# Sample attention of a hybrid decoder step: scores in the key matmuls, inverse key roots on GpSimd

## The chip, the cores and the metric

The kernel runs on one core of a Trainium2 chip, in one launch. The metric is the device time of that core in microseconds. The engines are named here as TensorE (PE in the profile; PEld are its weight loads), VectorE (DVE), ScalarE (ACT), GpSimd (POOL) and SyncE (SP).

## The reference

One inference step of a decoder layer over 1024 prompt tokens (plus 16 meta tokens) and over 8 running sequences of 8 new tokens each, which have 4096 cached positions. The part that this case is about is the attention of the sample tokens. Cached are latents `c` of 256 numbers and rotary keys `kr` of 32 numbers per position, in pages of 128 positions that a table names. For each of 8 heads:

```python
k_nope = einsum('tr,rhd->thd', c_all, w_uk)            # 64 per head
k = rms_norm(concat([k_nope, broadcast(kr_all)]), gain) # 96 per head
s = einsum('qhd,khd->hqk', q, k) * SCALE                # masked to past positions
p = softmax(s)
ctx = einsum('hqk,kr->qhr', p, c_all)                   # over latents
out = einsum('qhr,rhv->qhv', ctx, w_uv)
```

with `rms_norm(x) = x * rsqrt(mean(x*x) + 1e-6) * gain`. Everything is float32.

## The kernel before, in words

The program runs stage after stage, each a block that all engines leave together: constants, the front of the sample tokens (`front`), `sample_prepare`, `sample_attention`, `sample_values`, then the front of the prompt tokens, prompt attention, the merge and the MLP. The change touches the three `sample_` stages and the allocations in `program`.

Float32 products are made of rounded parts: an operand is split into a high part (rounded to TensorE's fp32r type) and a low part (the rest), and `three_pass` (L101) adds high x high, high x low and low x high; L103, L104 and L105 in the profile are its three matmuls, whoever calls it.

`sample_attention` (L617) never forms the keys for the scores. The query is multiplied with `w_uk` in `sample_prepare`, so that a score is a product of a latent with 256 numbers (`qt`), plus a rotary part (`qrz`), times the inverse root of the key's mean square. Only for that root are the keys themselves computed: a page of latents against `w_uk` (512 columns: 8 heads of 64), squared and summed per head.

The work goes in steps. A step handles one group `g` of four pages (GP = 4), a sequence has 8 groups (GS), and there are 64 groups (NG) in all; each engine runs its own function once per step, in program order, and semaphores tie them together. Different stages of a group are done in later steps: in step `g`,

- SP loads pages ahead into a ring of 16 groups (L657 to L671); a slot is loaded anew when TensorE has finished its context (`S["ctx"]`).
- TensorE (`pe_step`, L687) transposes the latents of group g (L728, L729), makes the rotary part of the scores of group g-1 (L744, L746), and for each of that group's four pages the key product (L755, six matmuls of 512 columns) and the scores (L762: high latents against 128 columns, the high and low queries; L763: low latents against 64 columns; two of each, for the two halves of the latent). After the second page comes the context of group g-12 (`context`, L688; LAG = 12): probabilities times latents, eight matmuls of 258 columns, four with low latents (L710) and four with high ones (L706).
- ScalarE (`act_step`, L773) makes the high parts of the transposed latents (L779, L780), copies the low half of the scores (L785), takes the square root of group g-2's variances (L789), squares each page's keys out of PSUM (L795, `sq`), makes the high parts of the latents for the context (L802), and, once per sequence, the exponential (L809) and the high part of the probabilities (L816). Its table holds either square root or exponential, and `ACT_TABLE_LOAD` in the trace is the switch.
- VectorE (`dve_step`, L818) makes the low parts (L824, L827), the reciprocal of the roots (L834), the sum of the score halves (L841, one operand in PSUM), the product with the roots (L844, both operands in SBUF), the sum of squares of each page (L860, `ss`), the low latents of the context (L868), the variance (L874 to L879); once per sequence the maximum over the pages (L855), the low parts of the probabilities (L888) and the division (L896, L898) after TensorE has folded the halves (L733).
- GpSimd (`pool_step`, L901) squares the rotary keys (L906) and once per sequence takes the maximum across partitions (L914) and subtracts it (L916, 2112 columns).

The order within each function is written out by hand. The first 16 steps are unrolled, the next 48 run as a hardware loop of three turns with 16 steps each (L680), and 13 steps (L683) finish without loading.

## Time and profile before

| what | value |
|---|---|
| median of 3 runs | 2402.58 us (2398.13 to 2405.45) |
| the profiled execution | 2399.88 us, its span 2398.1 us |
| TensorE busy | 2186.3 us (91%) |
| VectorE busy | 1327.1 us (55%) |
| ScalarE busy | 865.5 us (36%) |
| GpSimd busy | 178.0 us (7%) |
| sample attention, first page to last context | 91.6 to 775.3 us |

The span runs from the first to the last instruction. Busy time of TensorE counts matmuls as drawn, which overlap each other. The granted clock (PEclk) is the share of TensorE's full speed of 2.4 GHz: 1.00 is 2.4 GHz, and a stretch with a lower mean was partly at 1.2 GHz.

### The profile page before, as it was taken

What the parts mean: (1) busy time and instruction counts of PE and PEld (TensorE: products, weight loads), DVE (VectorE), ACT (ScalarE), POOL (GpSimd) and SP (SyncE); (2) the same over time, 40 slices, a digit from 0 to 9 for tenths busy, and PEclk for the clock granted to TensorE, in tenths of its full rate; (3) what the DMA queues carried; (4) which work ended last, traced back from release to release, by engine and by line L of the source; (5) the groups of instructions that cost most, each with busy time, mean ns of one, the idle gap of its engine ahead of it and who ended that gap; (6) DMA issues with size and microseconds to landing.
All of it is one profiled execution on the core that took longest, in us unless ns stands there. A gap on an engine that the chain in (4) does not pass through costs nothing. (4 is left out here: it accounts for less than half of the span.)

```text
span 2398.1 us, 35318 instructions
## 1 busy us (share of the span) xinstructions
PE 2186.3 (91%) x12338; PEld 1935.9 (81%) x12338; DVE 1327.1 (55%) x2307; ACT 865.5 (36%) x1650; POOL 178.0 (7%) x208
## 2 busy tenths in 40 slices
PE   4799999999994599699869999899999999999998
PEld 2688888888883378588759999788999999999997
DVE  3477887887884366566554232444544445444444
ACT  3245554555563255566552111332221112112111
POOL 0001110111011000234300000000000000000000
PEclk8799999999997699899969999999999999999999
DMA  2231222222200310000041111502111111111102
GB/s 100 78 90 48 60 59 59 60 60 57 60 26 1 128 37 17 16 5 1 1 124 36 45 36 32 171 1 71 37 52 52 35 50 38 52 35 52 49 21 79
DMA packets 134181, 121.83 MB, mean 51 GB/s; under 512 B 47335, under 2 KB 118984, under 8 KB 134015
## 3 DMA queue, kind: packets, MB, share of 16 engines
q1 hardware_dynamic: 132023, 114.15, 16.1%
q0 software_dynamic: 2000, 5.73, 0.7%
q8 instruction: 80, 1.31, 0.2%
q14 instruction: 78, 0.64, 0.1%
HBM read 113.09 MB, written 6.00 MB: 50 GB/s over the span
## 5 line engine op out<-in xcount | busy, mean ns | idle before, releaser
L103 PE MATMUL ps<-mh,f_w1h 128*128 128x384 f32 (+1 forms) x768 | 250.6, 326 | 0.0
L105 PE MATMUL ps<-mh,f_w1l 128*128 128x384 f32 (+1 forms) x768 | 250.5, 326 | 0.0
L104 PE MATMUL ps<-ml,f_w1h 128*128 128x384 f32 (+1 forms) x768 | 250.3, 326 | 0.0
L795 ACT ACTIVATE sq<-ps 128x512 f32<-128x512 f32 x256 | 152.0, 597 | 233.7 <-PE ps L105 211.3
L1842 DVE TENSOR_TENSOR oT<-oT,ps 128x512 f32<-128x512 f32 x256 | 171.5, 685 | 106.9 <-PE ps L105 106.9
L860 DVE TENSOR_REDUCE ss<-sq 128x8 f32<-128x512 f32 x256 | 171.0, 681 | 101.2 <-ACT sq L795 100.3
L1797 ACT ACTIVATE f_z<-ps 128x384 f32<-128x384 f32 (+1 forms) x96 | 45.6, 475 | 502.0 <-PE ps L105 502.0
L103 PE MATMUL ps<-w_ukh,cTh 128*128 128x512 f32 x512 | 216.5, 423 | 2.2 <-ACT sq L795 2.2
L104 PE MATMUL ps<-w_ukl,cTh 128*128 128x512 f32 x512 | 204.0, 398 | 0.0
L105 PE MATMUL ps<-w_ukh,cTl 128*128 128x512 f32 x512 | 203.9, 398 | 0.0
L104 PE MATMUL ps<-f_late_l,f_late_h 128*128 128x512 f32 x512 | 199.9, 390 | 0.0
L105 PE MATMUL ps<-f_late_h,f_late_l 128*128 128x512 f32 x512 | 199.8, 390 | 0.0
L103 PE MATMUL ps<-f_late_h 128*128 128x512 f32 x512 | 199.3, 389 | 0.0
L1822 DVE TENSOR_TENSOR f_z<-f_z 128x384 f32<-128x384 f32 (+1 forms) x96 | 51.6, 537 | 253.8 <-ACT f_z L1797 253.8
L103 PEld LDWEIGHTS ps<-mh,f_w1h 128*128 128x128 f32 x768 | 144.2, 188 | 1.9
L104 PEld LDWEIGHTS ps<-ml,f_w1h 128*128 128x128 f32 x768 | 144.2, 188 | 1.8
L105 PEld LDWEIGHTS ps<-mh,f_w1l 128*128 128x128 f32 x768 | 144.1, 188 | 0.0
L763 PE MATMUL ps<-qt,cTl 128*128 (+1 forms) x512 | 120.6, 247 | 0.0
L105 PEld LDWEIGHTS ps<-w_ukh,cTl 128*128 128x128 f32 x512 | 97.3, 190 | 23.8
L762 PE MATMUL ps<-qt,cTh 128*128 (+1 forms) x512 | 114.8, 265 | 0.0
L105 PEld LDWEIGHTS ps<-f_late_h,f_late_l 128*128 128x128 f32 x512 | 96.1, 188 | 20.2
L103 PEld LDWEIGHTS ps<-w_ukh,cTh 128*128 128x128 f32 x512 | 98.1, 192 | 17.0 <-ACT sq L795 2.5
(385 smaller groups left out, 4848.3 us busy)
## 6 DMA issues: line engine op xcount, KB each, us to landing
c_ring<-in_cache_kv_latent SPq DMA_DIRECT2D x256, 128.0 KB, 2.0
f_raw<-in_w_ff SPq DMA_DIRECT2D x32, 1024.0 KB, 5.2
m_raw<-in_w_in SPq DMA_DIRECT2D x20, 512.0 KB, 3.9
kr_ring<-in_cache_k_rope SPq DMA_DIRECT2D x256, 16.0 KB, 1.8
fp_x<-in_x_prompt SPq DMA_DIRECT2D x8, 512.0 KB, 3.5
nx_x<-in_x_prompt SPq DMA_DIRECT2D x8, 512.0 KB, 4.3
f_raw<-in_w_o SPq DMA_DIRECT2D x16, 256.0 KB, 5.1
oT<-in_x_prompt POOLq DMA_DIRECT2D x8, 512.0 KB, 7.0
```

The costliest lines, as they stand in the source:

```text
L103: nc.tensor.matmul(out, lh, rh, start=first, stop=False)
L104: nc.tensor.matmul(out, lh, rl, start=False, stop=False)
L105: return nc.tensor.matmul(out, ll, rh, start=False, stop=last)
L762: nc.tensor.matmul(sc, cTh[:, p1, rc, keys], qt[:, bass.ds(q_at, 2 * HQ)], start=False, stop=False)
L763: last = nc.tensor.matmul(sc[:, 0, :], cTl[:, p1, rc, keys], qt[:, bass.ds(q_at, HQ)], start=False, stop=j == GP - 1 and rc == 1)
L795: nc.scalar.activation(sq[:, j % 2, :], ps[:, 3 + j % 2, :], ACT.Square).then_inc(S["sq"], 1)
L860: nc.vector.tensor_reduce(ss[:, (k - 1) % 2, j * H:(j + 1) * H], sq[:, j % 2, :].rearrange("p (h d) -> p h d", d=NOPE), AX.X, ALU.add).the ...
L1797: nc.scalar.activation(z[:, a, 0:w], ps[:, 2 * par + a, 0:w], ACT.Relu).then_inc(S["relu"], 1)
L1822: nc.vector.tensor_tensor(z[:, a, 0:w], z[:, a, 0:w], z[:, a, 0:w], ALU.mult).then_inc(S["z"], 1)
L1842: nc.vector.tensor_tensor(part, part, ps[:, bank, :], ALU.add).then_inc(S["y"], 1)
```

## The change

1. The scores leave their own matmuls. The key weights and the queries of a sequence stand side by side in `wq`: 256 columns of weights (heads 0 to 3) and 64 of queries, for the high and the low part; heads 4 to 7 are in `w_late` with 256 columns. A page is twelve matmuls, six of 320 columns and six of 256 (`page`), into two PSUM banks, of which there are two pairs. VectorE copies a sequence's queries into `wq` once per sequence; GpSimd fills the weights in `sample_prepare`.
2. The rotary part is a `three_pass` of 256 columns of its own for group g, copied out by ScalarE (`rope`), and VectorE adds it to the scores page by page (`scores_and_norms`). TensorE's next page but one waits for this sum, where it waited for the square.
3. ScalarE's square root and VectorE's reciprocal are replaced by GpSimd: times 1/96, plus eps, to the power -0.5. GpSimd also multiplies the scores by the roots, which VectorE did.
4. The maximum is kept running by VectorE group by group (`most`), and across partitions it is taken by TensorE (a transpose, `turned`), VectorE (`top`), TensorE again (`spread`) and a ScalarE copy (`gmax`); GpSimd's all-reduce goes.
5. Subtraction of the maximum, exponential, high and low parts of the probabilities go in four pieces of eight pages. GpSimd makes the high parts instead of ScalarE; the subtraction is moved two steps later, the splitting one step later.
6. GpSimd makes the low latents for the context while pages are loaded; VectorE does it in the last 13 steps.
7. To make room, `rope` and `summed` lie in the tile of the gain `g_attn`, which `sample_values` loads again (512 KB) behind `w_uv`, and the ring of rotary keys is halved, so that SP waits in the first 16 steps for the groups eight before.

The diff, cut to its core:

```diff
@@ sample_prepare, GpSimd
+    for part, w in enumerate((B["w_ukh"], B["w_ukl"])):
+        for par in range(2):
+            nc.gpsimd.tensor_copy(B["wq"][:, par, :, part, 0:H // 2 * NOPE], f32(w[:, :, 0:H // 2 * NOPE]))
+        nc.gpsimd.tensor_copy(B["w_late"][:, :, part, :], f32(w[:, :, H // 2 * NOPE:H * NOPE]))
@@ sample_attention
+    HALF = H // 2 * NOPE
+    NP = 4
+    parts = [slice(2 * GP * i, 2 * GP * (i + 1)) for i in range(NP)]
...
+c_ring, kr_ring = sb("c_ring", [P, RING, GP, KV]), sb("kr_ring", [P, GS, GP, ROPE])
...
+rope = C["g_attn"][:, 0:2 * GP * HQ].rearrange("p (a n) -> p a n", a=2)
+summed = C["g_attn"][:, 2 * GP * HQ:4 * GP * HQ].rearrange("p (a n) -> p a n", a=2)
...
+prob_hl = sb("prob_hl", [P, NPAGE, 2, HQ], F32R)
...
+def kn_bank(j):
+    return 3 + 2 * (j % 2)
@@ SP
+            sp.dma_start(kr_ring[:, k % GS, j, :], krope[bass.ds(page, 1), :, :].rearrange("a p n -> p (a n)")
...
+        if k >= GS:
+            sp.wait_ge(S["krt"], k - GS + 1)
+            sp.wait_ge(S["krsq"], k - GS + 1)
@@ pe_step, context()
+        if gi % 2 == 0:
+            pe.wait_ge(S["prob_lo"], seq_of(lap, k, LAG) * NP + (gi // 2 + 1))
@@ pe_step
+    def page(j):
...
+        if j == 0:
+            pe.wait_ge(S["lo"], 2 * g)
+        if valid(2) or j >= 2:
+            pe.wait_ge(S["summed"], 4 * g + (j - 5))
...
+        keys = slice(j * P, (j + 1) * P)
+        a, b = ps[:, kn_bank(j), 0:HALF + HQ], ps[:, kn_bank(j) + 1, 0:HALF]
+        for rc in range(2):
+            hi, lo = cTh[:, p1, rc, keys], cTl[:, p1, rc, keys]
+            wa, wb = B["wq"][:, par, rc], B["w_late"][:, rc]
+            three_pass(nc, a, hi, lo, wa[:, 0, :], wa[:, 1, :], rc == 0, rc == 1)
+            last = three_pass(nc, b, hi, lo, wb[:, 0, :], wb[:, 1, :], rc == 0, rc == 1)
+        last.then_inc(S["kn"], 1)
...
+            pe.wait_ge(S["lo"], 2 * g)
+        if last_of(k, 4, valid):
+            pe.wait_ge(S["gmax"], seq_of(lap, k, 4) + 1)
...
+                last = nc.tensor.transpose(ps[:, rc, j * P:(j + 1) * P], c_ring[:, k, j, rc * P:(rc + 1) * P], C["ident"][:])
+        last.then_inc(S["transposed"], 1)
+    if valid(1):
+        page(0)
...
+    if loading:
...
+        nc.tensor.transpose(ps[:, 2, 0:P], kr_ring[:, k % GS, :, :].rearrange("p a b -> p (a b)"),
+                            C["ident"][:]).then_inc(S["krt"], 1)
...
+        page(1)
+    if valid(LAG):
+        context()
+    if maximum:
+        pe.wait_ge(S["lmax"], seq_of(lap, k, 3) + 1)
+        if loading:
+            pe.wait_ge(S["lo"], 2 * g + 2)
+        nc.tensor.matmul(ps[0:HQ, 0, 0:P], lmax[:, (k - 3) % RING // GS, :], C["ident"][:], start=True, stop=True
+                         ).then_inc(S["turned"], 1)
+    if valid(1):
+        page(2)
+    if loading:
...
+        pe.wait_ge(S["krlo"], g + 1)
...
+        hi, lo = (qrz[:, bass.ds((b * 2 + part) * GP * HQ, GP * HQ)] for part in range(2))
+        three_pass(nc, ps[:, 2, P:P + GP * HQ], krTh[:, k % 2, :], krTl[:, k % 2, :], hi, lo, True, True
+                   ).then_inc(S["rope"], 1)
+    if maximum:
+        pe.wait_ge(S["top"], seq_of(lap, k, 3) + 1)
+        nc.tensor.matmul(ps[:, 1, 0:HQ], top[:, 0:1].broadcast_to([HQ, P]), C["ident"][0:HQ, 0:HQ], start=True, stop=True
+                         ).then_inc(S["spread"], 1)
+    if valid(1):
+        page(3)
@@ act_step
+    def squares(j):
...
+        act.wait_ge(S["kn"], 4 * g + (j - 3))
+        if valid(2) or j >= 2:
+            act.wait_ge(S["ssq"], 4 * g + (j - 5))
+        nc.scalar.activation(sq[:, j % 2, :].rearrange("p (a n) -> p a n", a=2),
+                             ps[:, kn_bank(j):kn_bank(j) + 2, 0:HALF], ACT.Square).then_inc(S["sq"], 1)
...
+    def exponential(i):
...
+        piece = prob[:, ((k - 4) % RING) // GS, slice(parts[i].start, parts[i].stop + (i == NP - 1)), :]
+        act.wait_ge(S["shifted"], b * NP + (i + 1))
+        nc.scalar.activation(piece, piece, ACT.Exp).then_inc(S["exp"], 1)
...
-        nc.scalar.activation(sd[:, k % 2, :], var[:, k % 2, :], ACT.Sqrt).then_inc(S["sd"], 1)
...
+    squares(0)
+    if loading:
+        act.wait_ge(S["krt"], g + 1)
...
+        nc.scalar.activation(krTh[:, k % 2, :], ps[:, 2, 0:P], ACT.Copy).then_inc(S["krhi"], 1)
+    squares(1)
...
+    exponential(0)
+    squares(2)
+    exponential(1)
+    if last_of(k, 3, valid):
...
+        act.wait_ge(S["spread"], b + 1)
+        nc.scalar.activation(gmax[:, (k - 3) % RING // GS, :], ps[:, 1, 0:HQ], ACT.Copy).then_inc(S["gmax"], 1)
+    squares(3)
+    if loading:
+        act.wait_ge(S["rope"], g + 1)
...
+        nc.scalar.activation(rope[:, k % 2, :], ps[:, 2, P:P + GP * HQ], ACT.Copy).then_inc(S["ropec"], 1)
+    exponential(2)
+    exponential(3)
@@ dve_step
+    split = last_of(k, 5, valid)
+    def scores_and_norms(j):
+        if valid(1):
+            dve.wait_ge(S["sq"], 4 * g + (j - 3))
...
+            nc.vector.tensor_tensor(summed[:, p1, j * HQ:(j + 1) * HQ], ps[:, kn_bank(j), HALF:HALF + HQ],
+                                    rope[:, p1, j * HQ:(j + 1) * HQ], ALU.add).then_inc(S["summed"], 1)
+            nc.vector.tensor_reduce(ss[:, p1, j * H:(j + 1) * H], sq[:, j % 2, :].rearrange("p (h d) -> p h d", d=NOPE),
+                                    AX.X, ALU.add).then_inc(S["ssq"], 1)
+        if split:
+            dve.wait_ge(S["prob_hi"], seq_of(lap, k, 5) * NP + (j + 1))
+            nc.vector.tensor_tensor(prob_hl[:, parts[j], 1, :], prob[:, ((k - 5) % RING) // GS, parts[j], :],
+                                    f32(prob_hl[:, parts[j], 0, :]), ALU.subtract).then_inc(S["prob_lo"], 1)
...
+            dve.wait_ge(S["hi"], 2 * g + rc + 1)
...
+        if k % GS == 0:
...
+            q = B["qt"][:].rearrange("p b c s n -> p (b c s n)")[:, bass.ds(b * 4 * HQ, 4 * HQ)]
+            nc.vector.tensor_copy(B["wq"][:, k // GS, :, :, HALF:HALF + HQ],
+                                  f32(q).rearrange("p (c s n) -> p c s n", c=2, s=2)).then_inc(S["q"], 1)
...
+    scores_and_norms(0)
+    if loading:
+        dve.wait_ge(S["krhi"], g + 1)
+        nc.vector.tensor_tensor(krTl[:, k % 2, :], ps[:, 2, 0:P], f32(krTh[:, k % 2, :]),
+                                ALU.subtract).then_inc(S["krlo"], 1)
+    scores_and_norms(1)
+    if last_of(k, 3, valid):
...
+        dve.wait_ge(S["turned"], b + 1)
+        nc.vector.tensor_reduce(top[:], ps[0:HQ, 0, 0:P], AX.X, ALU.max).then_inc(S["top"], 1)
+    scores_and_norms(2)
+    if last_of(k, LAG, valid):
+        dve.wait_ge(S["ctx"], g + (1 - LAG))
+        nc.vector.tensor_copy(craw[:], ps[:, 7, 0:KV + 1]).then_inc(S["ctx_copied"], 1)
...
+        scores = prob[:, par, GP * gi:GP * (gi + 1), :]
+        dve.wait_ge(S["scaled"], g - 1)
...
+        nc.vector.tensor_tensor(most[:], scores if gi == 0 else most[:], scores, ALU.max).then_inc(S["most"], 1)
+        if gi == GS - 1:
...
+            nc.vector.tensor_tensor(most[:, 0:2, :], most[:, 0:2, :], most[:, 2:4, :], ALU.max).then_inc(S["pair"], 1)
...
+            nc.vector.tensor_tensor(most[:, 0, :], most[:, 0, :], most[:, 1, :], ALU.max).then_inc(S["pair"], 1)
...
+            nc.vector.tensor_tensor(lmax[:, par, :], most[:, 0, :],
+                                    B["s_new"][:].rearrange("p b n -> p (b n)")[:, bass.ds(b * HQ, HQ)],
+                                    ALU.max).then_inc(S["lmax"], 1)
+    scores_and_norms(3)
+    if valid(1):
...
+        nc.vector.tensor_reduce(krss[:, p1, :], krsq[:, p1, :, :], AX.X, ALU.add).then_inc(S["krss"], 1)
...
+        nc.vector.tensor_tensor(var[:, p1, :].rearrange("p (t h) -> p t h", h=H),
+                                ss[:, p1, :].rearrange("p (t h) -> p t h", h=H),
+                                krss[:, p1, :].unsqueeze(2).broadcast_to([P, GP, H]), ALU.add).then_inc(S["var"], 1)
@@ pool_step
+    if last_of(k, 5, valid):
...
+        for i in range(NP):
+            pool.wait_ge(S["exp"], b * NP + (i + 1))
...
+            nc.gpsimd.tensor_copy(prob_hl[:, parts[i], 0, :], prob[:, ((k - 5) % RING) // GS, parts[i], :]
+                                  ).then_inc(S["prob_hi"], 1)
...
-        nc.gpsimd.partition_all_reduce(gmax[:, par, :], lmax[:, par, :], P, RMAX).then_inc(S["gmax"], 1)
...
+        nc.gpsimd.tensor_tensor(krsq[:, k % 2, :, :], keys, keys, ALU.mult).then_inc(S["krsq"], 1)
...
+        pool.wait_ge(S["var"], g - 1)
...
+        nc.gpsimd.tensor_tensor(sd[:, k % 2, :], var[:, k % 2, :], inv_qk[:], ALU.mult).then_inc(S["mean"], 1)
...
+        nc.gpsimd.tensor_tensor(sd[:, k % 2, :], sd[:, k % 2, :], eps[:, 0:1].broadcast_to([P, GP * H]),
+                                ALU.add).then_inc(S["sd"], 1)
...
+        nc.gpsimd.tensor_tensor(rinv[:, k % 2, :], sd[:, k % 2, :], power[:], ALU.pow).then_inc(S["rinv"], 1)
+        pool.wait_ge(S["rinv"], g - 1)
...
+        scores = prob[:, par, GP * gi:GP * (gi + 1), :]
+        nc.gpsimd.tensor_tensor(
+            scores.rearrange("p t (h q) -> p (t h) q", h=H),
+            summed[:, k % 2, :].rearrange("p (n q) -> p n q", q=NNEW),
+            rinv[:, k % 2, :].unsqueeze(2).broadcast_to([P, GP * H, NNEW]), ALU.mult).then_inc(S["scaled"], 1)
...
+    if last_of(k, 4, valid):
...
+        for i in range(NP):
+            span = slice(parts[i].start, parts[i].stop + (i == NP - 1))
+            piece = prob[:, par, span, :]
+            nc.gpsimd.tensor_tensor(piece, piece,
+                                    gmax[:, par, :].unsqueeze(1).broadcast_to([P, span.stop - span.start, HQ]),
+                                    ALU.subtract).then_inc(S["shifted"], 1)
+    if valid(LAG - 1) and loading:
+        pool.wait_ge(S["c_hi"], g + (2 - LAG))
+        nc.gpsimd.tensor_tensor(cl[:, (k - LAG + 1) % 2, :, 0:KV], c_ring[:, (k - LAG + 1) % RING, :, :],
+                                f32(ch[:, (k - LAG + 1) % 2, :, 0:KV]), ALU.subtract).then_inc(S["c_lo"], 1)
@@ VectorE, before its steps
+    nc.vector.memset(eps[:], EPS).then_inc(S["const"], 1)
+    nc.vector.memset(inv_qk[:], 1.0 / QK).then_inc(S["const"], 1)
+    nc.vector.memset(power[:], -0.5).then_inc(S["const"], 1)
@@ sample_values, SP
+    sp.dma_start(C["g_attn"][:], row(A["g_attn"]).broadcast_to([P, D])).then_inc(gain_in, 16)
+    sp.wait_ge(gain_in, 16)
@@ program
+        "wq": sb("wq", [P, 2, 2, 2, H // 2 * NOPE + H * NNEW], F32R),
+        "w_late": sb("w_late", [P, 2, 2, H // 2 * NOPE], F32R),
```

## Rows read from the trace of the kernel before

**Rows 1.** Busy time by stretch: us, then PE, PEld, DVE, ACT, POOL, clock, DMA share, GB/s.
```profile
440.00:500.00 60.00, 60.00 (x372) 53.02 (x371) 48.29 (x94) 31.36 (x62) 2.72 (x7) 1.00 0.23 61
388.00:400.00 12.00, 9.12 (x40) 7.61 (x39) 4.62 (x11) 3.27 (x8) 0.40 (x1) 0.72 0.18 44
728.00:778.00 50.00, 17.75 (x90) 13.54 (x88) 22.05 (x26) 15.69 (x14) 6.26 (x3) 0.69 0.00 0
```

**Rows 2.** Timeline of PEld over one page: start, duration, engine, line, operation.
```profile
400.65 0.19 PEld L104 LDWEIGHTS ps<-w_ukl,cTh 128*128 128x128 f32 x1
400.88 0.19 PEld L105 LDWEIGHTS ps<-w_ukh,cTl 128*128 128x128 f32 x1
...
402.06 0.19 PEld L763 LDWEIGHTS ps<-qt,cTl 128*128 128x128 f32 x1
402.17 0.19 PEld L762 LDWEIGHTS ps<-qt,cTh 128*128 128x128 f32 x1
...
402.50 0.19 PEld L104 LDWEIGHTS ps<-w_ukl,cTh 128*128 128x128 f32 x1
```

**Rows 3.** Timeline of PEld, the first loads of two consecutive steps.
```profile
699.14 0.86 PEld L728 LDWEIGHTS ps<-ident,c_ring 128*128 128x128 f32 x8
...
708.74 0.86 PEld L728 LDWEIGHTS ps<-ident,c_ring 128*128 128x128 f32 x8
```

**Rows 4.** Timeline of PEld and PE at other widths of the moving operand (context; prompt front).
```profile
400.04 0.56 PEld L706 LDWEIGHTS ps<-ch,prob_hl 128*128 128x128 f32 x4
836.13 0.34 PE L103 MATMUL ps<-p_wlh,fp_xTh 128*128 128x384 f32 x1
...
836.65 0.29 PE L103 MATMUL ps<-p_wlh,fp_xTh 128*128 128x288 f32 x1
...
837.05 0.33 PE L103 MATMUL ps<-p_wlh,fp_xTh 128*128 128x384 f32 x1
```

**Rows 5.** Groups by line and shape, 450 to 500 us: busy, mean ns of one | idle before.
```profile
L795 ACT ACTIVATE sq<-ps 128x512 f32<-128x512 f32 x21 | 12.6, 598 | 20.3 <-PE ps L105 17.4 <-DVE ss L860 2.9
L868 DVE TENSOR_TENSOR cl<-c_ring,ch 128x1024 fp32r<-128x1024 f32 x5 | 6.1, 1224 | 1.1 <-ACT ch L802 1.1
L844 DVE TENSOR_TENSOR prob<-summed,rinv 128x256 f32<-128x256 f32 x6 | 2.5, 424 | 0.2
L906 POOL TENSOR_TENSOR krsq<-kr_ring 128x128 f32<-128x128 f32 x4 | 1.6, 400 | 36.8 <-DVE krss L874 36.8
```

**Rows 6.** Timeline of POOL and DVE around one subtraction of the maximum.
```profile
426.75 4.73 POOL L916 TENSOR_TENSOR prob<-prob,gmax 128x2112 f32<-128x2112 f32 x1 [7.11 <-issue]
427.27 0.42 DVE L841 TENSOR_TENSOR summed<-ps,low 128x256 f32<-128x256 f32 x1 [0.19 <-DVE rinv L834]
427.73 4.04 DVE L844 TENSOR_TENSOR prob<-summed,rinv 128x256 f32<-128x256 f32 x1
```

**Rows 7.** Timeline of POOL and of SP's queue in sample_prepare.
```profile
56.36 3.50 POOL L525 MEMSET qrz<- 128x4096 f32 x1
69.52 0.61 SPq L585 DMA_DIRECT2D qrz<-qrl  x1
```

**Rows 8.** Timeline of PE at the end of a sequence: [idle before <- releaser].
```profile
436.39 0.65 PE L733 MATMUL ps<-craw,fold 128*64 128x257 f32 x2 [1.43 <-DVE craw L885]
```

**Rows 9.** Timeline of DVE, POOL and PE at the end of the stage.
```profile
728.56 0.19 DVE L879 SCALAR_TENSOR_TENSOR var<-ss,krv 128x32 f32<-128x32 f32 x1
741.11 0.54 POOL L914 PARTITION_ALL_REDUCE gmax<-lmax  x1 [5.79 <-issue]
748.50 4.62 POOL L916 TENSOR_TENSOR prob<-prob,gmax 128x2112 f32<-128x2112 f32 x1 [6.85 <-issue]
760.18 0.56 PE L706 MATMUL ps<-ch,prob_hl 128*128 128x258 f32 x1 [18.74 <-DVE prob_hl L888]
```

**Rows 10.** DMA issues of the page: KB each, median us from issue to landing.
```profile
fp_x<-in_x_prompt SPq DMA_DIRECT2D x8, 512.0 KB, 3.5
```

More of the change, by code:

```diff
@@ L670, in _ @@
                     sp.wait_ge(S["ctx"], lap * RING + (k - RING + 1))
[L671 removed]
+                    load(k, lap * RING + k)
         def steps(emit):
@@ L685, in steps, with last_of, seq_of @@
             return program
+        def last_of(k, back, valid):
+            return (k - back) % GS == GS - 1 and valid(back)
+        def seq_of(lap, k, back):
+            return lap * 2 + (k - back) // GS
         def pe_step(pe, k, g, lap, valid, loading):
+            p1 = (k - 1) % 2
             def context():
@@ L899, in dve_finish @@
                                         ps[0:HQ, 7, 0:KV], rden[:, bass.ds(b, 1)], None, ALU.mult).then_inc(S["ctxn"], 1)
-        def pool_step(pool, k, g, lap, valid, loading):
+            if valid(LAG - 1) and not loading:
+                dve.wait_ge(S["c_hi"], g + (2 - LAG))
+                nc.vector.tensor_tensor(cl[:, (k - LAG + 1) % 2, :, 0:KV], c_ring[:, (k - LAG + 1) % RING, :, :],
+                                        f32(ch[:, (k - LAG + 1) % 2, :, 0:KV]), ALU.subtract).then_inc(S["c_lo_end"], 1)
```

263 lines of the change are left out of this document (95 added, 168 removed).

## The prediction

> **What bounds the kernel now.** I read the windows first. In a stretch of sample attention away from its turns, TensorE is busy all 60 of 60 us, VectorE 48.3, ScalarE 31.4 and GpSimd 2.7, at granted clock 1.00 [rows 1]. So TensorE is the bound there, and a change pays only through its instruction stream; the others matter where they make it wait. The second stretch of [rows 1] is a turn of the loop and the third the end of the stage, where TensorE works 17.75 of 50 us: a chain of latencies.
>
> Matmuls overlap in the records (one of 512 columns is drawn 0.40 long and the next begins 0.23 later), so I read TensorE's weight loads: each begins when the matmul before it starts to stream. From the second load of one page to the second of the next is 1.85 us: six key matmuls 0.23 apart (1.41) and four score matmuls 0.11 apart (0.44) [rows 2]. The score matmuls have only 128 and 64 columns, yet none is under 0.11. A whole step (one group of four pages, context included) is 9.60 us [rows 3]; four pages are 7.40, so transposes, rotary part and context are 2.20.
>
> **The change, part by part.** *Pages.* Now 6x512 + 2x128 + 2x64 = 3456 columns in ten matmuls; after, 6x320 + 6x256 = 3456 columns in twelve. The number of columns is the same: what goes is the floor under four short ones. Matmuls of 384 and 288 columns come 0.173 and 0.133 apart, 0.04 for 96 columns, so 320 is 0.147 and 256 is 0.120 by that line; the context's matmuls of 258 columns come at (0.56-0.19)/3 = 0.123 [rows 4]. The 512s of [rows 2] lie 0.007 above the same line (0.234 against 0.226), so I take 0.150 and 0.123: a page is 6x0.273 = 1.64, bounds 1.60 and 1.65. Saving 0.21 (0.20 to 0.25) x 256 pages = **54 us** (51 to 64). By the Trainium skill (TensorE: Matmul & The Clock Gate, "Wait — 56ns, not 53.3ns?") warm matmuls start N/2.4 GHz + 2.5 ns apart: 0.216 for 512 where the row has 0.234. By that rule the page would go from 1.74 to 1.47 and the saving be 69 us; the row speaks against so small a fixed cost here.
>
> *Rotary part.* 512+256 columns become three of 256: 0.234+0.12 against 0.37, +1 us over 64 steps. *The maximum by TensorE:* a transpose and a spread by plain fp32 matmuls, four instructions per sequence, est. 0.5 us (nearest rows: 0.12 each at least, doubled for an unrounded operand): +4 us, bounds 2 to 8.
>
> *ScalarE.* Works 31.4/60x9.6 = 5.0 us a step [rows 1]. Square root, low copy and the split copy of the probabilities go, a rotary copy of 256 columns comes: still 5, against a step of 9.60-4x0.21 = 8.76 after. Its table switches go too; in the steady part they are covered by TensorE's work, worth 0. Four pages' squares stay 0.6 each [rows 5].
>
> *VectorE.* 48.3/60x9.6 = 7.7. It gives up the low part of the latents (1.22 [rows 5]) and the 256-wide product with the roots (0.42 [rows 5]), and gets a 256-wide maximum (0.42) and four adds of 64 columns instead of one of 256 (0.42 for that one [rows 6], so at most 0.42 each): at most 7.7-1.22-0.42-0.42+0.42+1.68 = 7.7, under 8.76. Its stand of 4 us at a sequence's end goes too: in [rows 6] the product takes 4.04 while GpSimd's 4.73 us shift runs, where it needs 0.42, and an add with one operand in PSUM, inside the same shift, keeps its 0.42.
>
> *GpSimd.* It becomes a busy engine. Cost per element from 0.40 us for 128 [rows 5] and 4.73 for 2112 [rows 6]: 2.18 ns, and 0.12 fixed. A step: squares of rotary keys 0.40; times 1/96 and plus eps, 32 wide, 0.19 each; the power, X; product 256 wide 0.68; low latents 1024 wide 2.35; a sequence's shift 4.73+3x0.12 over eight steps 0.64; rounding copy of 2048, between a fill's 3.50/4096 [rows 7] and the two-operand 2.18 per element, 1.7 to 4.5, so 0.2 to 0.55. Sum 4.9 and some 0.1 of waits: **5.0+X**. It bounds the step only if X is over 3.8. No row shows a power. Lower bound: a plain operation of 32 columns, 0.19; upper bound: none in these rows, the longest GpSimd operation is 4.73. I take 1 us, nearer to the small operation because the operand is as small; both ends stay for the cases.
>
> *Waits.* GpSimd's product for group k-2 is done some 5 us into TensorE's step; VectorE asks for it (the maximum) after the third page, about 8.8. Behind that wait on VectorE stands the fourth page's add, which frees the bank for the second page of the next step; that has 1.7 us to spare. So covered, if X is small. At a sequence's end the covers go: the first context matmul waits for a GpSimd copy, then VectorE's split, and that stands behind two latent splits, reciprocal, scaling and a page's norms on VectorE: ready about 1.9 us late by my laying out of the step. GpSimd, after shift and copies, gives the product at about 8.7+X-1, right where its 2.35 us latent operation follows: about 0.9 more. Now each of the seven inner ends has one gap, 1.15 to 2.15, in sum 11.2; [rows 8] shows one of 1.43. After, about 2.8 each, 20 in sum: +8 to +10, of which I count **+8**, and +3 for a clock dip or two. The loop's two turns (12 us with 2.9 idle and mean clock 0.72 [rows 1], so 6.7 us at the 1.2 GHz level) stay.
>
> *End of the stage.* From the last variance (728.75) to the first context matmul of the last sequence (760.18) are 31.4 us; GpSimd waits 5.79 before the all-reduce and 6.85 before the shift for nothing recorded [rows 9]. After: scale, eps, power, product 2.3; maxima 1.3; transpose, reduce, spread and copy 1.6 (four hops, est. 0.4); four shifts 5.1; copy 0.9; split 0.6; and 1 of order between engines = 13. Saving **18** (12 to 20). The 15 us of contexts behind it stay.
>
> *Hidden edits.* GpSimd's six weight copies (512 wide, 0.6 to 1.2 each) start after its 3.50 us fill at 60 and end by 64 to 67, while SP still issues rotary queries at 69.52 [rows 7]; without that cover they cost up to 7. The gain's reload, 512 KB, stands behind the value weights in SP's queue while TensorE multiplies them; a load of that size takes 3.5 [rows 10] and that, uncovered, is its price. SP's waits for the halved rotary ring look eight groups back: 0.
>
> **Sum.** -54+1+4+8+3-18 = -56 against the profiled execution's 2399.88: 2344; the median of the runs is 2.7 above that execution, so **2346.5**. Its own range: pages -64, turns +2, no loss at the ends and -20 give 2323; pages -51, end -12, turns +8 and ends +15 give 2362.
>
> **Rivals.**
> A, *the sequence ends cost more and cool TensorE.* Two waits at each of seven ends become 3 us longer than counted and each brings a dip like the loop turn's: (3+3.4)x7 = 45, less the 11 counted: 2381. For it: GpSimd and VectorE hand work back and forth three times there. Against: a gap of 1.43 was followed by 60 us at clock 1.00 [rows 1, 8]. Chance 0.17.
> B, slower: *GpSimd becomes the bound through the power.* Its step is 5.0+X; beyond X = 3.8 each us costs 64, and the whole gain of 56 is gone at 4.6. With X = 6: 2346.5+64x2.2 = 2490. If the power needed code brought in each time, as the 5.8 and 6.9 us before the present GpSimd pair look like [rows 9], it would be hundreds more. For: no row prices it, and four operations follow one another. Against: it has 32 columns. Chance 0.10.
> C, *the lock.* If GpSimd's 2.35 us operation starts just before VectorE's maximum in every step, the maximum, which has both operands in SBUF, ends 2.4 late, and the second page 0.9 late: 64x0.9 = +58, 2404, no change. The rows show such a block once per sequence [rows 6]; against it, the operation should start at 6.2, after the latents' copy, and be over at 8.6. The Trainium skill (SBUF — State Buffer, "Who interferes with whom") says that VectorE with two SBUF inputs and a reading GpSimd exclude each other for a whole instruction; by that rule, the trace agrees. Chance 0.05.
> That the "one table" part does nothing by itself I take as given.
>
> **Numbers.** Forecast case 0.68, A 0.17, C 0.05, B 0.10. A measurement here tells 0.3% (7 us) from no change. Faster takes the forecast, A and part of C: 0.87; same 0.03; slower 0.10. The range goes from the forecast's low end, 2323, to A with its clock dips, 2385; B and most of C lie outside.
>
> **What would show it.** Weight loads of a page 1.64 apart in all; a step of 8.8; the power's duration on GpSimd under 3.8 and GpSimd busy about 6 of 8.8; VectorE's maximum 0.4 long and not 2.8; gaps on TensorE at sequence ends before the first context matmul, released by the split; 13 us from last variance to first context. A step over 9.3, or idle TensorE in every step, would prove the forecast wrong.

## The result and the profile after

| what | before | after |
|---|---|---|
| median | 2401.18 us (2398.13 to 2405.45, 4 runs) | 2494.24 us (2492.31 to 2495.48, 4 runs) |
| span of the profiled execution | 2398.1 us | 2491.9 us |
| GpSimd busy | 178.0 us (7%) | 741.6 us (30%) |

The kernel became slower: ratio 1.0386, 95% interval 1.0367 to 1.0404. The forecast was 2346.5, range 2323 to 2385; the chance of slower was put at 0.10.

First the page of the profile after, its engines and the costliest group:

```profile
PE 2186.3 (88%) x12946; PEld 1987.3 (80%) x12946; DVE 1277.4 (51%) x2369; ACT 828.9 (33%) x1596; POOL 741.6 (30%) x603
...
L992 POOL TENSOR_TENSOR rinv<-sd,power 128x32 f32<-128x32 f32 x64 | 351.8, 5497 | 5.0
...
L103 PE MATMUL ps<-wq,cTh 128*128 128x320 f32 x512 | 179.7, 351 | 96.6 <-DVE g_attn_b L884 95.9
```

L992 is the power: 5.50 us for 32 columns, on which the forecast had spent 1. TensorE's busy time is that of before, in spite of shorter pages, in part because it ran sample attention at a lower clock (0.94 against 0.99, below); and there are 96 us in which it waits for the sum of the scores (`summed`, L884, which lies in the tile `g_attn_b`).

The windows answer to [rows 1]: us, then PE, PEld, DVE, ACT, POOL, clock, DMA share, GB/s. The second goes from the first full steps to the last variance, the third from there to the first context matmul of the last sequence.

```profile
440.00:500.00 60.00, 50.83 (x339) 47.68 (x338) 37.91 (x81) 26.10 (x50) 50.35 (x42) 0.90 0.18 46
103.00:826.30 723.30, 602.92 (x4217) 573.82 (x4216) 451.97 (x955) 312.38 (x588) 612.16 (x455) 0.94 0.19 50
826.30:848.60 22.30, 6.95 (x25) 4.65 (x25) 9.19 (x15) 5.51 (x8) 16.50 (x17) 0.60 0.00 0
```

The same two stretches of the kernel before:

```profile
103.00:728.50 625.50, 608.54 (x3637) 529.08 (x3635) 499.96 (x904) 344.93 (x641) 64.09 (x82) 0.99 0.22 58
728.50:760.20 31.70, 5.60 (x21) 3.90 (x21) 12.15 (x15) 9.34 (x8) 6.26 (x3) 0.58 0.00 0
```

So the stage lost 97.8 us up to the last variance, got 9.4 back at its end, and the rest of the program is 5.4 longer: together the 93.8 by which the spans differ. TensorE is idle 120.4 us of the long stretch, against 17.0. GpSimd works 50.35 of 60 us and not 60: it is heavily loaded, but something else closes the ring. The timeline of one step shows it; first GpSimd:

```profile
455.98 0.40 POOL L979 TENSOR_TENSOR krsq<-kr_ring 128x128 f32<-128x128 f32 x1 [1.85 <-DVE krss L955]
456.33 0.25 POOL L987 TENSOR_TENSOR sd<-var,inv_qk 128x32 f32<-128x32 f32 x1
456.66 0.24 POOL L989 TENSOR_TENSOR sd<-sd,eps 128x32 f32<-128x32 f32 x1
456.98 5.44 POOL L992 TENSOR_TENSOR rinv<-sd,power 128x32 f32<-128x32 f32 x1
462.66 0.63 POOL L999 TENSOR_TENSOR prob<-g_attn_b,rinv 128x256 f32<-128x256 f32 x1 [0.23 <-POOL rinv L992]
463.25 2.19 POOL L1020 TENSOR_TENSOR cl<-c_ring,ch 128x1024 fp32r<-128x1024 f32 x1
466.79 0.40 POOL L979 TENSOR_TENSOR krsq<-kr_ring 128x128 f32<-128x128 f32 x1 [1.34 <-DVE krss L955]
```

Then VectorE, in the same step:

```profile
463.48 2.24 DVE L942 TENSOR_TENSOR most<-prob 128x256 f32<-128x256 f32 x1 [1.92 <-POOL prob L999]
465.65 0.21 DVE L884 TENSOR_TENSOR g_attn_b<-ps,g_attn_b 128x64 f32<-128x64 f32 x1
465.78 0.67 DVE L886 TENSOR_REDUCE ss<-sq 128x8 f32<-128x512 f32 x1
466.37 0.27 DVE L955 TENSOR_REDUCE krss<-krsq 128x4 f32<-128x128 f32 x1
```

From one L979 to the next are 10.81 us, where a step was 9.60 [rows 3]. The ring: GpSimd makes scale, eps, power and product (to 463.29); VectorE's running maximum has waited for that product, and starts 0.23 us after GpSimd's low latents (L1020), so it takes 2.24 instead of 0.42; behind it stand the fourth page's add, for which TensorE waits, the page's reduction and `krss`; and GpSimd may begin its next step only after `krss`. GpSimd is idle 1.3 to 2.8 us before L979 in nearly every round; in the one behind a sequence's copies it isn't.

The saving on the pages came. PEld over one page of the changed kernel, which answers to [rows 2]:

```profile
458.32 0.19 PEld L104 LDWEIGHTS ps<-wq,cTh 128*128 128x128 f32 x1
...
459.12 0.19 PEld L104 LDWEIGHTS ps<-wq,cTh 128*128 128x128 f32 x1
...
459.92 0.19 PEld L104 LDWEIGHTS ps<-qrz,krTh 128*128 128x128 f32 x1
```

Half a page, six matmuls, is 0.80 us (458.32 to 459.12 to 459.92), a page 1.60.

### The profile page after: what moved, and what is told of

The parts are those of the page before. It is cut to its first block and busy times, and to the rows that moved or that the text cites. A ratio compares the mean times of both kernels' runs of the same rounds, so it can differ in the third digit from the quotient of the medians.

```text
span 2491.9 us, 37255 instructions
## 1 busy us (share of the span) xinstructions
PE 2186.3 (88%) x12946; PEld 1987.3 (80%) x12946; DVE 1277.4 (51%) x2369; ACT 828.9 (33%) x1596; POOL 741.6 (30%) x603
## 5 line engine op out<-in xcount | busy, mean ns | idle before, releaser
L992 POOL TENSOR_TENSOR rinv<-sd,power 128x32 f32<-128x32 f32 x64 | 351.8, 5497 | 5.0
L103 PE MATMUL ps<-wq,cTh 128*128 128x320 f32 x512 | 179.7, 351 | 96.6 <-DVE g_attn_b L884 95.9
L103 PEld LDWEIGHTS ps<-wq,cTh 128*128 128x128 f32 x512 | 102.5, 200 | 113.5 <-DVE g_attn_b L884 107.4
L105 PE MATMUL ps<-wq,cTl 128*128 128x320 f32 x512 | 164.4, 321 | 0.0
L104 PE MATMUL ps<-wq,cTh 128*128 128x320 f32 x512 | 163.9, 320 | 0.0
L105 PE MATMUL ps<-w_late,cTl 128*128 128x256 f32 x512 | 148.9, 291 | 0.0
L104 PE MATMUL ps<-w_late,cTh 128*128 128x256 f32 x512 | 148.7, 290 | 0.0
L103 PE MATMUL ps<-w_late,cTh 128*128 128x256 f32 x512 | 148.6, 290 | 0.0
```

The costliest lines, as they stand in the source:

```text
L103: nc.tensor.matmul(out, lh, rh, start=first, stop=False)
L104: nc.tensor.matmul(out, lh, rl, start=False, stop=False)
L105: return nc.tensor.matmul(out, ll, rh, start=False, stop=last)
L992: nc.gpsimd.tensor_tensor(rinv[:, k % 2, :], sd[:, k % 2, :], power[:], ALU.pow).then_inc(S["rinv"], 1)
```

## The experiments

The theories: *place*, the power hurts through the ring just read, and moving what stands in it helps; *capacity*, GpSimd simply has too much to do and moving VectorE's work changes nothing; and, for what is left without the power, *lock* (two engines block each other) against *order* (VectorE reaches the split late). Each group of runs has its own time of the kernel before, from the same chip: 2393.91 us for e1, e3, e4 and e5, 2406.27 for e2, e8, e9 and e10 (all of these are single executions, and the kernel of e2_sqrt, run twice, gave ratios of 0.9706 and 0.9755, so that under 0.5% they tell nothing), and 2400.89, a median, for e12 to e15, which are medians of four runs.

### The power alone

**e1_mult.** The power becomes a product of the same 32 columns, so the inverse roots are left out; everything else stands as in the changed kernel.

```diff
-nc.gpsimd.tensor_tensor(rinv[:, k % 2, :], sd[:, k % 2, :], power[:], ALU.pow).then_inc(S["rinv"], 1)
+nc.gpsimd.tensor_tensor(rinv[:, k % 2, :], sd[:, k % 2, :], power[:], ALU.mult).then_inc(S["rinv"], 1)
```

> The power on GpSimd becomes a product of the same 32 columns, so the roots are not taken; everything else of the change stays. If the power's 5.44 us are the whole cause, GpSimd's work per sequence falls from about 85 us to 43 and every wait behind it is covered: 2340 to 2360 us, as was forecast for a cheap power. If something else in the new layout costs as much (the two lost sequence-end gaps, the clock, the queries beside the weights), it stays over 2400. The step on TensorE should be 8.6 to 8.8 us.

Measured: 2367.66 us, 26.3 below before. So without the power all of the loss is gone and most of the missing gain is there, but the time is above what was expected. The long stretch and the end (windows of e1_mult):

```profile
103.00:706.90 603.90, 564.40 (x4217) 551.91 (x4216) 397.75 (x956) 311.93 (x588) 281.63 (x453) 0.97 0.24 60
706.90:724.00 17.10, 7.42 (x25) 4.75 (x25) 9.17 (x15) 5.49 (x8) 11.32 (x17) 0.54 0.00 0
```

TensorE is idle 39.5 us, 22.5 more than before, at clock 0.97. The long gaps are at the sequence ends; timeline of DVE, POOL and PE around one:

```profile
487.14 5.19 POOL L1015 TENSOR_TENSOR prob<-prob,gmax 128x512 f32<-128x512 f32 x4
...
491.31 0.22 DVE L884 TENSOR_TENSOR g_attn_b<-ps,g_attn_b 128x64 f32<-128x64 f32 x1 [2.45 <-ACT sq L826]
...
492.28 2.19 POOL L1020 TENSOR_TENSOR cl<-c_ring,ch 128x1024 fp32r<-128x1024 f32 x1
492.38 2.38 DVE L942 TENSOR_TENSOR most<-most,prob 128x256 f32<-128x256 f32 x1
...
495.71 1.80 DVE L960 TENSOR_TENSOR var<-ss,krss 128x32 f32<-128x32 f32 x1
...
499.50 2.17 POOL L1020 TENSOR_TENSOR cl<-c_ring,ch 128x1024 fp32r<-128x1024 f32 x1
500.06 2.16 DVE L890 TENSOR_TENSOR prob_hl<-prob,prob_hl 128x512 fp32r<-128x512 f32 x1
...
502.27 0.58 PE L737 MATMUL ps<-ch,prob_hl 128*128 128x258 f32 x1 [4.79 <-DVE prob_hl L890]
```

Three VectorE instructions with both operands in SBUF are held while GpSimd works: the maximum (0.42 when free), the variance (0.19 when free, here beside GpSimd's rounding copies) and the split (0.68 when free), while L884, with one operand in PSUM, keeps 0.22 inside the four pieces of the shift, 5.19 us together. Six of the seven inner ends cost TensorE 4.75 to 4.88 us each, the first one 3.28.

**e5_halfpow.** The power for 16 of the 32 columns, a product for the other 16 (half of the roots are left out).

```diff
+nc.gpsimd.tensor_tensor(rinv[:, k % 2, 0:GP * H // 2], sd[:, k % 2, 0:GP * H // 2], power[:, 0:GP * H // 2], ALU.pow)
+nc.gpsimd.tensor_tensor(rinv[:, k % 2, GP * H // 2:], sd[:, k % 2, GP * H // 2:], power[:, GP * H // 2:], ALU.mult).then_inc(S["rinv"], 1)
```

> The power is taken of 16 of the 32 columns, the other 16 are multiplied in an instruction of their own, so half the roots are not taken. If a power costs per column (0.17 us), it lasts 2.7 to 2.8 us, the ring is 8.2 to 8.4 us with the block, under TensorE's 8.6, and the total 2350 to 2370 us. If its 5.44 us are fixed per instruction, it lasts 5.4 again and the total stays at 2490 to 2510.

Measured: 2369.24 us, 1.6 above e1_mult and inside the 2350 to 2370 of a price per column. The group by line and shape:

```profile
L992 POOL TENSOR_TENSOR rinv<-sd,power 128x16 f32<-128x16 f32 x64 | 190.0, 2969 | 5.0
```

Against 5497 ns for 32 columns that is 0.158 us per column, and 0.44 fixed. A power of 3 us is as good as free, which fits the forecast's bound of 3.8; one of 5.5 costs 119 us against none (93.1 above its before for the changed kernel, 26.3 below for e1_mult).

### Place or capacity

**e3_maxlate.** The maximum's block in `dve_step` is moved unchanged from before the fourth page's norms to behind the variance; the power stays.

```diff
-if valid(2):
-    kk = (k - 2) % RING
...
 scores_and_norms(3)
 if valid(1):
...
                         krss[:, p1, :].unsqueeze(2).broadcast_to([P, GP, H]), ALU.add).then_inc(S["var"], 1)
+if valid(2):
+    kk = (k - 2) % RING
...
```

> VectorE's running maximum, which waits for GpSimd's product, moves from in front of the fourth page's add to the end of VectorE's step, behind the variance. The power stays. Theory place (a ring: variance, power, product, maximum, fourth page, next variance, 10.8 us a step where GpSimd's own work is about 9.2 to 10.6): the ring is cut, a sequence falls from 94.9 us to 86 to 88, the total to 2430 to 2450 us. Theory capacity (only GpSimd's sum of work counts): no change, 2480 to 2495 us.

Measured: 2421.57 us, 27.7 above before, where the changed kernel is 93 above. Between 440 and 500 us:

```profile
440.00:500.00 60.00, 53.44 (x383) 50.32 (x384) 47.70 (x92) 30.56 (x57) 57.84 (x46) 0.97 0.20 53
```

That is even below the 2430 to 2450 of *place* and far from the 2480 to 2495 of *capacity*. With the ring cut GpSimd works 57.84 of 60 us, and its steps come 9.64 apart: now it is full, and being full costs 54 us over e1_mult. The other 65 of the changed kernel were the place. The lock itself is still there, but off the ring: at its new place the maximum is held in more than half of the steps. One of them, timeline of DVE:

```profile
466.16 2.42 DVE L953 TENSOR_TENSOR most<-most,prob 128x256 f32<-128x256 f32 x1
```

**e4_lowdve.** The low latents (L1020) go from GpSimd to VectorE behind the second page's norms; the power and the maximum's place stay.

```diff
 scores_and_norms(1)
+if valid(LAG - 1) and loading:
+    dve.wait_ge(S["c_hi"], g + (2 - LAG))
+    nc.vector.tensor_tensor(cl[:, (k - LAG + 1) % 2, :, 0:KV], c_ring[:, (k - LAG + 1) % RING, :, :],
+                            f32(ch[:, (k - LAG + 1) % 2, :, 0:KV]), ALU.subtract).then_inc(S["c_lo"], 1)
```

> The low latents of the context go back from GpSimd to VectorE in all steps, after the second page. The power and the maximum's place stay. GpSimd loses 2.2 us a step, and nothing is left that blocks VectorE's maximum behind the product. Theory place: the ring is 10.8 less the 1.8 us of blocking = 9.0 to 9.1 us, still over TensorE's 8.6: 2370 to 2390 us. Theory capacity: GpSimd's work is about 67 us a sequence, 8.4 a step, TensorE is the bound: 2345 to 2360 us. If neither the block nor GpSimd's sum counts: 2480 to 2495.

Measured: 2389.24 us, 4.7 below before, which one execution can't tell from no change, and inside the 2370 to 2390 of *place*. The ring is still there but free of the lock (timelines of POOL and DVE):

```profile
453.94 0.40 POOL L983 TENSOR_TENSOR krsq<-kr_ring 128x128 f32<-128x128 f32 x1 [1.53 <-DVE krss L959]
...
454.95 5.44 POOL L996 TENSOR_TENSOR rinv<-sd,power 128x32 f32<-128x32 f32 x1
456.79 1.21 DVE L925 TENSOR_TENSOR cl<-c_ring,ch 128x1024 fp32r<-128x1024 f32 x1
460.64 0.64 POOL L1003 TENSOR_TENSOR prob<-g_attn_b,rinv 128x256 f32<-128x256 f32 x1 [0.25 <-POOL rinv L996]
462.79 0.40 POOL L983 TENSOR_TENSOR krsq<-kr_ring 128x128 f32<-128x128 f32 x1 [1.52 <-DVE krss L959]
```

A round is 8.85 us against 10.81, so 1.96 less; the maximum alone is 1.8 shorter. Not all of it is the lock, since this edit also takes 2.2 us of work a step from GpSimd, and e3_maxlate shows that with this work GpSimd needs 9.64 a round in any case: over that, ring and lock added 1.17. 8.85 is just over TensorE's own step (8.67, below).

The second and third line show something else: VectorE's low latents, both operands in SBUF, run inside the power and take 1.21 us, as they do when GpSimd is idle (1.22 [rows 5]). All 53 of this line (L925) took 1.21 to 1.23. So the power does not shut VectorE out. What is held in these runs is held beside GpSimd's plain operations.

**e15_power_free.** Both edits together, power kept.

> The changed kernel with its power kept on GpSimd, but with both edits of e3_maxlate and e4_lowdve together: the maximum behind the variance, and the low part of the latents on VectorE. GpSimd then has 0.40+0.25+0.24+5.44+0.63 = 7.0 us a step and about 8 us a sequence besides, 8.0 a step in all, under TensorE's 8.6. If the price of the power is GpSimd's time and the ring it closes, that price is gone but for the ends: 2360 to 2380. If something else in the power costs TensorE or VectorE (a port, the clock), it stays at 2390 or above.

Measured: 2374.05 us (2372.75 to 2376.04), ratio 0.9891, interval 0.9875 to 0.9908: the ratio of e1_mult to its before (2367.66/2393.91 = 0.989). Between 190 and 250 us:

```profile
190.00:250.00 60.00, 60.00 (x466) 58.97 (x465) 46.65 (x110) 33.30 (x64) 49.93 (x37) 1.00 0.27 71
```

TensorE is busy 60 of 60 in this stretch, beside powers of 5.44 us. Up to the last variance it is idle 40.0 us at clock 0.97, where e1_mult, without the power, has 39.5 at 0.97. So no cost of the power to TensorE or VectorE is left to be seen; the price was GpSimd's time and the ring.

### The roots on other engines

**e2_sqrt.** The power and GpSimd's two small operations go; ScalarE takes the square root straight after the first page's squares, with scale 1/96 and bias eps in the same instruction, and VectorE the reciprocal after the first page's norms. Product and low latents stay on GpSimd.

```diff
 squares(0)
+if valid(2):
+    act.wait_ge(S["var"], g - 1)
+    nc.scalar.activation(sd[:, k % 2, :], var[:, k % 2, :], ACT.Sqrt, scale=1.0 / QK, bias=eps[:, 0:1]).then_inc(S["sd"], 1)
...
 scores_and_norms(0)
+if valid(2):
+    dve.wait_ge(S["sd"], g - 1)
+    nc.vector.reciprocal(rinv[:, k % 2, :], sd[:, k % 2, :]).then_inc(S["rinv"], 1)
```

> GpSimd's three steps to the root go; ScalarE takes the square root again (of the variance times 1/96 plus eps in the same instruction) and VectorE the reciprocal. Everything else of the change stays, the low latents on GpSimd too. Theory: the power was the price and ScalarE's table was never one: as with the power made a product, 2360 to 2375 us, the two table loads of 1.28 us a sequence costing at most 10 in all. If the single table is what matters in the new layout, it is over 2390.

Measured: 2335.45 us beside 2406.27, 25 us below the expected range, so it was timed again as **e12_sqrt_again**:

> The same kernel as e2_sqrt, timed again beside the others of this call so that they can be compared on one chip: 0.965 to 0.975 of before, some 2333 us. Both theories expect the same.

Measured: 2343.22 us (2339.45 to 2345.21), ratio 0.9755, interval 0.9739 to 0.9771. It beats both kernels. PEld, first loads of the context in two consecutive steps, 8.67 apart:

```profile
449.00 0.49 PEld L741 LDWEIGHTS ps<-cl,prob_hl 128*64 128x64 f32 x4
...
457.67 0.50 PEld L741 LDWEIGHTS ps<-cl,prob_hl 128*64 128x64 f32 x4
```

And its windows:

```profile
103.00:683.30 580.30, 559.48 (x4213) 547.02 (x4211) 392.18 (x1017) 340.63 (x660) 243.43 (x267) 0.98 0.24 63
683.30:701.40 18.10, 6.41 (x25) 4.11 (x25) 9.57 (x16) 8.21 (x11) 9.68 (x14) 0.69 0.00 0
```

TensorE is idle 20.8 us up to the last variance, against 39.5 in e1_mult, though the inverse roots are computed here and ScalarE switches its table for every exponential and back (15 loads of 1.28 us). A sequence's end, DVE, POOL and PE:

```profile
483.73 1.15 DVE L966 TENSOR_TENSOR var<-ss,krss 128x32 f32<-128x32 f32 x1
...
487.43 0.76 DVE L895 TENSOR_TENSOR prob_hl<-prob,prob_hl 128x512 fp32r<-128x512 f32 x1
488.11 0.34 DVE L925 RECIPROCAL rinv<-sd 128x32 f32<-128x32 f32 x1
...
488.69 0.64 POOL L996 TENSOR_TENSOR prob<-g_attn_b,rinv 128x256 f32<-128x256 f32 x1 [0.24 <-DVE rinv L925]
...
488.25 0.38 PE L737 MATMUL ps<-ch,prob_hl 128*128 128x258 f32 x1 [1.75 <-DVE prob_hl L895]
```

The gap is 1.75 where e1_mult has 4.79 (1.75 to 1.87 at six of the seven inner ends, 3.42 at the first). GpSimd's product now waits for VectorE's reciprocal, which stands right behind the split; so the low latents, which follow the product, can't start before the split is over, and it takes 0.76 and not 2.16. And the variance, though still held 1.15, is over 1.6 us before TensorE's gap begins (484.88; the gap begins at 486.50), where in e1_mult it ends as the gap begins (497.51 and 497.48). At this end the two add up to the 3 us (1.40 and 1.62); no run changed one of them alone.

**e8_lnexp.** As e2_sqrt, but the inverse root as exp(-0.5 ln x), both on ScalarE.

```diff
+nc.scalar.activation(sd[...], var[...], ACT.Ln, scale=1.0 / QK, bias=eps[:, 0:1]).then_inc(S["sd"], 1)
+act.wait_ge(S["sd"], g - 1)
+nc.scalar.activation(rinv[...], sd[...], ACT.Exp, scale=-0.5).then_inc(S["rinv"], 1)
```

> The roots as exp(-0.5 ln(x/96 + eps)), two ScalarE instructions of 32 columns, no square root, no power, no reciprocal. If logarithm and exponential lie in one table, there are no table loads inside the stage: 2360 to 2372 us, equal to or up to 5 us under the square root. If they lie in two, there are two loads of 1.28 us in every step on ScalarE, which has 3 us to spare: 2365 to 2400.

Measured: 2402.35 us, beside 2406.27 for before and 2335.45 for e2_sqrt; just over the 2400 that two loads a step were given at most. Groups of ScalarE between 190 and 690 us, by line:

```profile
L850 ACT ACT_TABLE_LOAD x49 | 62.9, 1283 | 0.9
L852 ACT ACT_TABLE_LOAD x49 | 62.9, 1283 | 0.9
```

The logarithm and the exponential each bring a load in every step: 2.57 us on ScalarE ahead of the rotary copy, for which VectorE's split of the rotary keys and then TensorE wait. TensorE's steps are 9.19 us where e2_sqrt's are 8.66, some 34 us in 64 steps, and its waits for the split of the probabilities at the sequence ends are up to 4.5 us. The Trainium skill (ScalarE: Activation LUTs, "Table sets: the hidden batching unit") says that one set holds both functions, so that ln and then exp need one load. As this program was compiled they took one each, 98 in the stretch; whether it can be made to use one set was not tried.

**e9_lnexp_low** (e8_lnexp with the low latents on VectorE, the edit of e4_lowdve) and **e10_early** (that, with the first split at the head of VectorE's step).

> The run before, and the low latents of the context go back to VectorE. Theory lock: at a sequence's end VectorE's operations with two operands in SBUF (maximum 2.38, variance 1.80, split 2.16 us, where they need 0.42, 0.2 and 0.65) stand behind GpSimd's 2.2 us latents, which makes TensorE's gap of 4.8 us and its dip to the 1.2 GHz level. Without them the gap is 1 to 2.5 us, the time at the lower level falls from 61 us to 15 to 30, and the total is 2325 to 2345 us. Theory order (VectorE's own queue is too long there; the lock is a detail): the 1.2 us more of work on VectorE keep the gap over 4 us and the total at 2360 to 2380.

> The run before, and the first piece's split stands at the head of VectorE's step, before the two latent splits, the division and the first page. Theory lock: the gap before the first context matmul goes to under 0.7 us, 0 to 15 us less than the run before. Theory order: this is the step that closes the gap, 15 to 35 us less than the run before.

Measured: 2420.98 and 2416.76 us. The first is far above all that was expected; the second is 4.2 below the first, which falls in the 0 to 15 of *lock*, but is less than two single executions can tell apart. The table loads weigh most here and the question of lock or order isn't answered: in the waits of e9_lnexp_low between 190 and 800 us,

```profile
POOL prob L1001 <- ACT rinv L852: 221.4, 54, 11.7
DVE krTl L927 <- ACT krTh L857: 103.2, 52, 2.5
```

GpSimd waits up to 11.7 us for the roots and VectorE 2 us a step for the rotary copy. So the two edits were made again on e2_sqrt.

### Lock or order at the ends

**e14_sqrt_lowdve.** e2_sqrt with the edit of e4_lowdve.

> e2_sqrt with the low part of the latents (1024 wide) on VectorE after the second page instead of on GpSimd: the power, the lock through this operation and the table loads of the logarithm are all absent, which was not so in e9_lnexp_low. If the 2.2 us GpSimd operation still holds VectorE up at the sequence ends (lock), 2325 to 2333. If it is the fullness of VectorE that counts (1.22 us more in each of its steps of about 8.6), the ends get later: 2340 to 2360.

Measured: 2338.29 us (2333.83 to 2339.72), ratio 0.9734, interval 0.9718 to 0.9750, beside 0.9755 (0.9739 to 0.9771) for e12_sqrt_again, the kernel of e2_sqrt: 4.9 us less at the median, but the intervals overlap, so that the two can't be told apart. TensorE is idle 20.1 us up to the last variance against 20.8, and the gap at an end stays (1.78, on the same releaser). The window:

```profile
103.00:677.00 574.00, 553.87 (x4219) 541.61 (x4217) 448.62 (x1071) 342.52 (x661) 129.09 (x215) 0.99 0.24 63
```

2338 lies in neither forecast. Both were counted from 2333 for e2_sqrt, which took 2343 here; from that, the run is on the lock's side. But the gap that it was to explain has not shrunk: with the product behind the reciprocal, the low latents are no longer what makes it. What differs is TensorE's clock, 0.99 over this stretch against 0.98 in e12_sqrt_again, some 6 us. It comes and goes with one and the same kernel: e2_sqrt's execution, with the same gaps, had 0.99 too. So the 4.9 us can't be credited to the edit. VectorE, at 48.5 of 60 us, can carry the low latents.

**e13_sqrt_early.** e2_sqrt with the first split ahead of the latent splits.

```diff
+if split:
+    dve.wait_ge(S["prob_hi"], seq_of(lap, k, 5) * NP + 1)
+    nc.vector.tensor_tensor(prob_hl[:, parts[0], 1, :], prob[:, ((k - 5) % RING) // GS, parts[0], :],
+                            f32(prob_hl[:, parts[0], 0, :]), ALU.subtract).then_inc(S["prob_lo"], 1)
 if loading:
     for rc in range(2):
         dve.wait_ge(S["hi"], 2 * g + rc + 1)
```

> e2_sqrt with the first of a sequence's four splits of the probabilities at the head of VectorE's step, ahead of the two latent splits, instead of behind page 0's norms. If the gap of 1.7 to 1.9 us before the first context matmul at each of seven sequence ends is VectorE's order, it goes, at most 7 x 1.8 = 13 us: 2320 to 2328, with a little more if clock dips go with it. If the split waits there for GpSimd's copy and not for its turn on VectorE, it now holds up the latent splits instead, and the time stays or gets worse: 2333 to 2345.

Measured: 2359.88 us (2358.52 to 2367.24), ratio 0.9828, interval 0.9811 to 0.9844: worse even than the second forecast, also when that is counted from 2343. VectorE at an end:

```profile
417.50 2.62 DVE L900 TENSOR_TENSOR prob_hl<-prob,prob_hl 128x512 fp32r<-128x512 f32 x1 [0.68 <-POOL prob_hl L982]
420.04 1.28 DVE L905 TENSOR_TENSOR cTl<-ps,cTh 128x512 fp32r<-128x512 f32 x2
...
421.54 0.47 DVE L919 TENSOR_SCALAR c_new<-ps,rden 64x256 f32 x1 [0.15 <-DVE rden L917]
```

Moved ahead, the split waits 0.68 for GpSimd's copy and then runs beside GpSimd's other copies, 2.62 instead of 0.76; behind it come the latent splits and the division, which the context matmul needs as well. TensorE's gap becomes 3.84 at this end, released by the division. The order of before was the better one.

## Why the prediction was wrong

**The step that failed** is the one that priced the power: "I take 1 us, nearer to the small operation because the operand is as small". It is 5.50 on average, and 5.44 undisturbed: 29 times the 0.19 of a plain operation that was the lower bound. The working itself had no upper bound, and said so; with nothing above it, the smallness of the operand was no reason, since e5_halfpow shows that the price is per element of a costly function, 0.158 us a column where a product costs some 0.002. By the working's own 64 us for each us of X over 3.8, the range of 2323 to 2385 left out every X over 4.4, although the case beyond had been worked out.

**Rival B** came true, with its place (GpSimd) and its order of operations. That its figure (2490 for X = 6) is so near to 2494 is luck. By its own formula X = 5.44 gives 2346.5 + 64 x 1.64 = 2451, and the runs divide the way to 2494 otherwise (each against its own before, put on the scale of 2401.18): 28 us are lost in e1_mult, without any power (2375 against 2346.5); 54 more when GpSimd is full but the ring is cut (e3_maxlate); 65 more through the place of the maximum, ring and lock together. The formula had 105 for the full GpSimd. It set GpSimd's mean step, sequence work included, against TensorE's undisturbed 8.76, while the mean step of e1_mult, ends and turns included, is 9.64 and that of e3_maxlate 10.41 (from the first L979 to the last).

**Rival C**, the maximum held behind GpSimd's low latents, is part of those 65, and the working had it apart from B. C was priced at 0.9 us a step; ring and lock together add 1.17 a round over GpSimd's own work (10.81 against e3_maxlate's 9.64), and 1.96 go when the low latents leave GpSimd (e4_lowdve). Each was judged against the slack that the other one took away: with a cheap power C does nothing in a plain step (e1_mult's steps are 8.65 apart), and with a dear power it is still there, but off the ring, once the maximum has moved (e3_maxlate). With the ring but without this work on GpSimd, the power costs 22 us over none (e4_lowdve); no run has the ring and the work without the lock. The Trainium skill (SBUF — State Buffer, "Who interferes with whom") states the lock as a rule on operands in SBUF; by that rule, the traces agree beside GpSimd's plain operations: L884 keeps 0.22 us, while L942, L960 and L890 stretch to 2.38, 1.80 and 2.16. Beside the power they do not: L925 of e4_lowdve takes its free 1.21 inside it, and the measurement decides.

**The pages**, -54 (51 to 64): a page is 1.60, the lower bound, and a step of TensorE 8.67 in e12_sqrt_again against 8.76 forecast. The step fell by 0.93, times 64 is 59.5. Right, 6 us too low in size. The saving of 69 us by the rule of the Trainium skill (TensorE: Matmul & The Clock Gate, "Wait — 56ns, not 53.3ns?") is not the rule's alone: the 1.74 of before has the rows' 0.11 for each short matmul in it. By the rule alone, an estimate, the page would be 1.47 before and after; measured are 1.85 and 1.60. The ends of the range, added from the terms named, are 2322 and 2364 where it has 2323 and 2362; nothing hangs on it.

**The ends**, +8 and +3 for the clock, and **rival A**: read from e1_mult, where the power costs no more than the forecast took. Gaps of 4.8 instead of 2.8, idle time up by 22.5 instead of 8, and clock 0.97 instead of 0.99 over 604 us, some 12 us at full speed. On the scale of 2401.18 the run would be 2375, between the forecast and A (2381), inside the range; e5_halfpow, whose power takes 2.97, is within 2 us of it, so a power of 1 us would have done the same. The working had the alternation of VectorE and GpSimd but not that three of VectorE's instructions there would be locked out.

**The end of the stage**, 13 us and a saving of 18 (12 to 20): 17.1 in e1_mult where it was 31.7, so a saving of 14.6, in the range; 22.3 in the changed kernel, which is that and the power once. The four shifts took 6.07 instead of 5.1, and each of GpSimd's four copies has an operation on one element, 0.18 us, before it (L971), which the working left out.

**Hidden edits.** Weight copies, the gain's reload and SP's waits at the halved ring: the first transposes of the stage come at 81.6 where they came at 82.7, so the copies at least are covered. From the first context matmul of the last sequence to the end are 1641.8 us in e1_mult against 1637.9 before, where the reload was counted at nothing. But e2_sqrt has 1637.3 and e12_sqrt_again, the same kernel with the same reload, 1642.0: what the reload costs is less than these executions differ by.

**One table on ScalarE** was put at nothing, and was less than nothing in these runs: the version that keeps switching tables is 1.4% below the best one that doesn't (0.9755 for e12_sqrt_again, 0.9891 for e15_power_free, and as much for e1_mult, without roots). But more than the tables differs: the order of work at the sequence ends too, and it is there that TensorE loses less, 20.8 us idle up to the last variance against 40.0 and 39.5.

## What to carry over

An operation that no row prices can't be forecast by the size of its operand; if the sum breaks at some X, and nothing bounds X, much of the chance belongs to the case beyond. When work moves to GpSimd, draw the ring of who waits for whom over a whole step, and look in it for VectorE instructions with both operands in SBUF: beside GpSimd's plain operations three of them were stretched to 1.8 to 2.4 us, though not beside its power, and in a ring that length is paid every time. ScalarE's two table loads a sequence, in the shadow of TensorE, cost less than the detour that avoids them; two in every step cost more than it (e8_lnexp at 0.998 of before, e15_power_free at 0.989).
